# GpSimd sums the softplus of later key blocks: one product with ones per block row in a two-layer decoder trunk

## What is computed

```python
mask = k_pos[None, :] < q_pos[:, None]
z = jnp.einsum('bhqd,bhkd->bhqk', q_blk, k).astype(jnp.float32) * scale
log_beta = jax.nn.log_sigmoid(z)
log_stay = jnp.where(mask, jax.nn.log_sigmoid(-z), 0.0)
log_remain = lax.cumsum(log_stay, axis=3, reverse=True) - log_stay
w = jnp.where(mask, jnp.exp(log_beta + log_remain), 0.0)
return jnp.einsum('bhqk,bhkd->bhqd', w.astype(v.dtype), v)
```

## Time and profile before

| | |
|---|---|
| median of three runs | 4052.87 us |
| the profiled execution | 4055.05 us, of which the span is 4053.0 us |
| TensorE busy (matmuls) | 3955.4 us, 98% of the span |
| VectorE busy | 2637.8 us, 65% |
| ScalarE busy | 1431.2 us, 35% |
| GpSimd busy | 1285.3 us, 32% |
| mean granted TensorE clock | 0.988 of full speed |

### The profile page before, as it was taken

The page is one execution under the profiler, slowest core; times in us unless marked ns, Lnnn a source line. Parts: engine busy times, 40 slices in busy tenths (PEclk is TensorE's granted clock), DMA queues, the critical chain, the costliest instruction groups (busy, mean ns, idle before and its releaser), DMA issues.

```text
span 4053.0 us, 57462 instructions
## 1 busy us (share of the span) xinstructions
PE 3955.4 (98%) x18186; PEld 3240.2 (80%) x18186; DVE 2637.8 (65%) x4343; ACT 1431.2 (35%) x1891; POOL 1285.3 (32%) x869
## 2 busy tenths in 40 slices
PE   8999999999999999999889999999999999999998
PEld 5777878888888878888667777888888888788885
DVE  5742548967774278888566436388777732878784
ACT  4533233333333333333344433333333333333333
POOL 0100003433331077676001000044333310777750
PEclk9999999999999999999999999999999999999999
DMA  3222223445454599999212222234445446999991
GB/s 110 69 87 89 99 78 125 141 158 192 171 186 144 190 341 370 350 356 339 79 64 78 83 93 99 73 131 145 174 171 190 167 146 204 346 366 365 351 322 63
DMA packets 323751, 740.17 MB, mean 183 GB/s; under 512 B 30496, under 2 KB 161696, under 8 KB 319904
## 3 DMA queue, kind: packets, MB, share of 16 engines
q1 hardware_dynamic: 104400, 381.73, 26.9%
q10 hardware_dynamic: 174160, 222.40, 16.2%
q0 software_dynamic: 45056, 134.38, 9.0%
HBM read 618.87 MB, written 119.54 MB: 182 GB/s over the span
## 4 chain that ended last, share of the span: by engine, by line
PE 93%; DVE 2%; issue 2%; ACT 1%; DMA 0%; POOL 0%; ACTq 0%; DVEq 0%; POOLq 0%; SPq 0%
PE bank L1071 60%; PE bank L1279 24%; PE bank L1259 4%; PE bank L1135 1%; PE bank L1125 1%; PE bank L1143 1%; DVE xl L708 1%; PE bank L1092 1%; DVE rs L701 0%; PE bank L1120 0%; PE bank L1214 0%; PE bank L1213 0%; PE bank L1212 0%; DMA vrow<-in_stream,tail_v 0%; ACTq L621 0%
## 5 line engine op out<-in xcount | busy, mean ns | idle before, releaser
L1071 PE MATMUL bank<-xh,hi 128*128 128x512 f32 x3264 | 1311.4, 402 | 42.2 <-DVE xl L708 42.1
L1071 PE MATMUL bank<-xl,hi 128*128 128x512 f32 x3264 | 1277.0, 391 | 0.0
L1071 PE MATMUL bank<-xh,lo 128*128 128x512 f32 x3264 | 1276.4, 391 | 0.0
L696 DVE TENSOR_TENSOR lo<-raw,hi 128x1024 fp32r<-128x1024 f32 (+1 forms) x532 | 642.7, 1208 | 643.4 <-ACT hi L432 596.8
L432 ACT ACTIVATE hi<-raw 128x1024 fp32r<-128x1024 f32 x724 | 739.1, 1044 | 278.9 <-DMA raw<-in_stream 173.9
L380 POOL TENSOR_TENSOR lo<-raw,hi 128x1024 fp32r<-128x1024 f32 x192 | 481.5, 2508 | 1002.4 <-ACT hi L432 1002.2
L1071 PEld LDWEIGHTS bank<-xh,hi 128*128 128x128 f32 x3264 | 616.1, 189 | 194.7 <-DVE xl L708 59.6
L1071 PEld LDWEIGHTS bank<-xh,lo 128*128 128x128 f32 x3264 | 615.9, 189 | 130.6
L1071 PEld LDWEIGHTS bank<-xl,hi 128*128 128x128 f32 x3264 | 617.0, 189 | 120.3 <-issue 3.8
L392 POOL DMA_INDIRECT hval<-early,tail_h x256 | 397.6, 1553 | 428.2 <-DMA early<-eo 347.2
L1279 PE MATMUL bank<-hi,ah 128*128 128x512 f32 x1536 | 475.1, 391 | 12.0 <-DVE al L995 10.3
(11 more groups left out here) (195 smaller groups left out, 3436.6 us busy)
## 6 DMA issues: line engine op xcount, KB each, us to landing
raw<-in_stream SPq DMA_DIRECT2D x724, 512.0 KB
early<-eo ACTq DMA_DIRECT2D x256, 256.0 KB, 2.2
gate_table<-stage ACTq DMA_DIRECT2D x24, 2048.0 KB, 7.4
gb<-gate_table ACTq DMA_DIRECT2D x64, 768.0 KB
eb<-early ACTq DMA_DIRECT2D x64, 768.0 KB
hval<-early,tail_h POOLq DMA_INDIRECT x256
vrow<-in_stream,tail_v POOLq DMA_INDIRECT x256
hT<-in_xT ACTq DMA_DIRECT2D x2, 1024.0 KB, 6.8
```

What stands on the lines that cost most here:

```text
L696: dve.tensor_tensor(lo[k % RING][:, 0:w], raw[k % RAW][:, 0:w], hi[k % RING][:, 0:w].bitcast(f32), ALU.subtract).then_inc(lo_split, 1)
L1071: ins = pe.matmul(out_ap, st[slot][:, a:a + P], mv, start=first and i == 0, stop=last and i == 2)
```

## The change

GpSimd, after its four softplus masks, builds two sums per head: `laterS[1]` (256 columns: block 2 over queries 256 to 383, and blocks 2 + 3 over the last 128) and `laterS[0]` (384 columns: block 1 over queries 128 to 255, and block 1 plus `laterS[1]` over the rest). That is a copy and an add of 128 columns, then a copy of 128 and an add of 256. ScalarE rounds both sums (`laterH`), VectorE takes the rests (`laterL`). TensorE uses them for block rows 1 and 0 in place of one product per later block; rows 3 and 2 are as before. VectorE's `attSl` of blocks 3 and 2 now waits for the first sum and that of block 1 for the second, because it overwrites `attS` that GpSimd still reads.

```diff
--- before.py
+++ after.py
@@ -168,6 +168,9 @@
     attS = sb("attS", o_r + 8 * KB, [P, NBLK, SEQ])
     attW = sb("attW", o_r, [P, NBLK, SEQ])
     attSh = sb("attSh", o_r + 16 * KB, [P, NBLK, SEQ], f32r)
+    laterS = [sb("laterS0", o_r + 6 * KB, [P, 384]), sb("laterS1", o_r + 4 * KB, [P, 256])]
+    laterH = [sb("laterH0", o_r + 22 * KB, [P, 384], f32r), sb("laterH1", o_r + 20 * KB, [P, 256], f32r)]
+    laterL = [sb("laterL0", o_r + 6 * KB, [P, 384], f32r), sb("laterL1", o_r + 4 * KB, [P, 256], f32r)]
     attSl = sb("attSl", o_r + 8 * KB, [P, NBLK, SEQ], f32r)
     qb = sb("qb", o_r + 24 * KB, [P, SEQ])
     kb = sb("kb", o_r + 26 * KB, [P, SEQ])
@@ -267,6 +270,7 @@
         z_ready, abs_ready, ln_ready, sp_ready = sem("z_ready"), sem("abs_ready"), sem("ln_ready"), sem("sp_ready")
         sp_masked, arg_ready, w_ready, w_masked = sem("sp_masked"), sem("arg_ready"), sem("w_ready"), sem("w_masked")
         sp_hi, sp_lo, signs_ready = sem("sp_hi"), sem("sp_lo"), sem("signs_ready")
+        later_ready, later_hi, later_lo = sem("later_ready"), sem("later_hi"), sem("later_lo")
         pv_ready, pv_taken = sem("pv_ready"), sem("pv_taken")
         pooled, pooled_hi, pooled_lo = sem("pooled"), sem("pooled_hi"), sem("pooled_lo")
 
@@ -358,6 +362,16 @@
                         pool.wait_ge(sp_ready, a + i + 1)
                         apart(pool)
                         keep_later(attS, s, sp_masked)
+                    r = l * (4 * PAIRS) + h * 2
+                    pool.wait_ge(sp_masked, a + 3)
+                    apart(pool)
+                    pool.tensor_copy(laterS[1][:, 0:P], attS[:, 2, 2 * P:3 * P])
+                    pool.tensor_tensor(laterS[1][:, P:2 * P], attS[:, 2, 3 * P:SEQ], attS[:, 3, 3 * P:SEQ], ALU.add)\
+                        .then_inc(later_ready, 1)
+                    pool.tensor_copy(laterS[0][:, 0:P], attS[:, 1, P:2 * P])
+                    pool.wait_ge(later_ready, r + 1)
+                    pool.tensor_tensor(laterS[0][:, P:3 * P], attS[:, 1, 2 * P:SEQ], laterS[1][:, :], ALU.add)\
+                        .then_inc(later_ready, 1)
                     for i, s in enumerate(reversed(range(NBLK))):
                         pool.wait_ge(w_ready, a + i + 1)
                         apart(pool)
@@ -493,6 +507,9 @@
                         for i, s in enumerate(reversed(range(NBLK))):
                             act.wait_ge(sp_masked, a + i + 1)
                             act.activation(attSh[:, s, s * P:SEQ], attS[:, s, s * P:SEQ], ACT.Copy).then_inc(sp_hi, 1)
+                        for i in range(2):
+                            act.wait_ge(later_ready, (s2 + h) * 2 + i + 1)
+                            act.activation(laterH[1 - i][:, :], laterS[1 - i][:, :], ACT.Copy).then_inc(later_hi, 1)
                         split(l, 7 if h == 0 else 9, b)
                         if h:
                             act.wait_ge(pooled, l * PAIRS + b + 1)
@@ -768,8 +785,14 @@
                                                      attE[:, s, s * P:SEQ], ALU.max, ALU.add).then_inc(sp_ready, 1)
                         for i, s in enumerate(reversed(range(NBLK))):
                             dve.wait_ge(sp_hi, a + i + 1)
+                            if s:
+                                dve.wait_ge(later_ready, s1 * 4 + h * 2 + (2 if s == 1 else 1))
                             dve.tensor_tensor(attSl[:, s, s * P:SEQ], attS[:, s, s * P:SEQ],
                                               attSh[:, s, s * P:SEQ].bitcast(f32), ALU.subtract).then_inc(sp_lo, 1)
+                        for i in range(2):
+                            dve.wait_ge(later_hi, s1 * 4 + h * 2 + i + 1)
+                            dve.tensor_tensor(laterL[1 - i][:, :], laterS[1 - i][:, :], laterH[1 - i][:, :].bitcast(f32),
+                                              ALU.subtract).then_inc(later_lo, 1)
 
                     def turn_v():
                         dve.wait_ge(v_turned, s1 + 1)
@@ -1130,10 +1153,18 @@
                         a = s1 * 8 + h * 4
                         for i, s in enumerate(reversed(range(NBLK))):
                             pe.wait_ge(sp_lo, a + i + 1)
-                            for j in range(s, NBLK):
+                            for part in (attSh, attSl):
+                                ins = pe.matmul(bank[4 + s][:, s * P:SEQ], tri_r[:, :], part[:, s, s * P:SEQ],
+                                                start=False, stop=True, skip_group_check=True)
+                            if s == 2:
                                 for part in (attSh, attSl):
-                                    ins = pe.matmul(bank[4 + s][:, j * P:SEQ], (tri_r if j == s else ones_r)[:, :],
-                                                    part[:, j, j * P:SEQ], start=False, stop=True, skip_group_check=True)
+                                    ins = pe.matmul(bank[4 + s][:, 3 * P:SEQ], ones_r[:, :], part[:, 3, 3 * P:SEQ],
+                                                    start=False, stop=True, skip_group_check=True)
+                            if s < 2:
+                                pe.wait_ge(later_lo, s1 * 4 + h * 2 + 2 - s)
+                                for part in (laterH, laterL):
+                                    ins = pe.matmul(bank[4 + s][:, (s + 1) * P:SEQ], ones_r[:, :], part[s][:, :],
+                                                    start=False, stop=True, skip_group_check=True)
                             ins.then_inc(arg_ready, 1)
 
                     def weigh(h):
```

## The result

The changed kernel takes 4063.0 us (4060.24 to 4064.28, 11 runs). Beside it the kernel before took 4051.88 us (4050.0 to 4053.78, 11 runs). The ratio is 1.0027 with a 95% interval of 1.0017 to 1.0036: 11.1 us slower, 0.27%. 19.1 us were forecast. The profiled execution took 4061.87 us with a span of 4060.1 us, 7 us more than the profiled one of before. One execution of each says less than eleven, so times are compared by their medians, and the traces are used for where time goes. Followed from product to product, the two traces come 11.4 us apart in the attention, and back by 3.8 us in the stages between.

A forecast was written before the change was run, and what follows sets the result against it. TensorE was taken to bound the kernel, with 93% of the chain. Lateness in `remain`, 16.9 us with the saving counted, plus 2.2 us of `y` waits made 19.1 us slower: 4072.0 us, range 4060 to 4084 us, 8 in 10.

The forecast's parts named there:

- The gain of the products: TensorE's saved products in block rows 1 and 0 of `remain`: 0.57 us a head, 9.1 us in all, the ceiling.
- the step that the prediction called the deciding one: In `remain`, VectorE in order waits for GpSimd's second sum and TensorE for VectorE: 1.10 and 1.01 us late, 16.9 us.
- M: Start of GpSimd's mask of block 0, the last softplus mask of a head: 63.34 in head 0, 79.09 in head 1.
- the rival for the full gain: GpSimd's sums hidden in `remain`, L no later than M + 1.15: 9.1 us faster, about 4044 us; chance 0.02.
- The wait for `y`: TensorE waits for VectorE's `y` at the next pair's mix 0: 0.37 us, 6 times, 2.2 us.
- The clock rival: New waits in the attention bring back the low clock: at most 58 us on top, some 4130 us; chance 0.03.
- L: When VectorE sees GpSimd's second sum and starts `attSl` of block 1 in `remain`: M + 2.78.
- second sum alone: End of GpSimd's second sum for `remain`, with nothing disturbing it: M + 2.49.
- disturbance of GpSimd: GpSimd's copy and add slowed by VectorE's `attSl` of blocks 3 and 2: 0.25 us, bounds 0 and 0.5 us.
- the cheap rival: GpSimd's adds in proportion to columns, copies 0.2 us, no disturbance: L at M + 1.81, about 4056 us; chance 0.12.
- The term behind L: VectorE's remaining rests and TensorE's last products, from L until TensorE leaves `remain`: 2.73 us, at M + 5.51.
- The signs in the trace: TensorE waits in `remain` about 1.6 us a head for `attSl` of block 1 and `laterL[1]`; `remain` lasts about 3.8 us.

The follow-up runs named there:

- The fills: Changed kernel with GpSimd's two copies and two adds per head replaced by two fills with zero, synchronisation kept: 4045.12 us, ratio 0.9984.

## Why the prediction was right in direction and 8 us too dear

**Right.** The gain of the products was of the size predicted (9.1 us against 10.8 measured alone; the saving per head is 0.65 us where its rows gave 0.57), and it was lost at the step that the prediction called the deciding one: VectorE waits for GpSimd's second sum in its order, and TensorE waits for VectorE. The fills show that with that sum at M + 0.91 the gain is there; the rival for the full gain put its point at M + 1.15. The wait for `y` arose six times, as said. `pw` cost nothing. The granted clock did not fall in the attention: it is 1.00 from 63 to 120 us, and the wait of 0.59 us cost 0.06 us of restart. The clock rival's mechanism does exist in this kernel, but at waits of 4.43 us.

The measured 4063.0 us is inside the range given, 3 us from its low end and 9 us from the forecast.

**Wrong: the terms ahead of L.** This is where the sum was mis-sized, and every term of GpSimd's was too high.

| term | predicted | measured |
|---|---|---|
| mask to copy, copy to add | 0.33, 0.33 us | 0.24, 0.27 us |
| add of 128 columns (next start) | 0.62 us | 0.45 us (0.40) |
| second copy (next start) | 0.33 us | 0.25 us |
| add of 256 columns | 0.88 us | 0.77 us |
| second sum alone | M + 2.49 | M + 1.93 |
| disturbance of GpSimd | 0.25 us | 0 |
| VectorE late for the second sum | 0 | 0.18 us |

The straight line through the adds of 512 and 1024 columns gave a fixed part of 0.37 us and 0.62 us for 128 columns; 0.45 us was measured. Two far points don't fix the short end. In proportion to the columns, the cheap rival's way, 0.35 and 0.69 us were too low. The truth lay between, a little nearer to the cheap end. The estimate from the Trainium skill's figure for 2048 elements (GPSIMD Engine Reference, section 3.1) was 0.84 us for both adds. The trace has 1.22 us, so the estimate came 0.38 us too low, and the rows' 1.50 us 0.28 us too high.

**Wrong: who is disturbed.** I charged GpSimd 0.25 us for VectorE's rests of blocks 3 and 2. GpSimd wasn't slowed at all: in all 16 heads its longest second add is 0.79 us. Its add starts at 64.59, the rest of block 2 comes behind it, and that one takes 954 ns where it took 418. TensorE's first wait, 0.25 us, is for just this. The direction follows the order, as the third turn of the choice shows with waits of 4.43 us. The Trainium skill says it outright (SBUF — State Buffer, section Who interferes with whom): VectorE with two inputs in SBUF and GpSimd reading SBUF hold one shared port pair in turn, and whichever issues second "fully blocks". It also says that a GpSimd instruction that only writes doesn't contend. By this rule, the trace agrees: 0.954 us beside the add. Beside the fills the rest of block 3 took 0.292 us and that of block 2, whose start falls into the second fill, 0.418 us, as in the kernel before.

VectorE comes to the rest of block 1 at about 65.58, worked out from the start of `laterL` at 66.65 less the pitches of blocks 0 and 1 (0.61 and 0.46 us). So L was M + 2.15 where I had M + 2.78, 0.63 us too late. The second sum was there at M + 1.93 and seen some 0.04 us later; the last 0.18 us of L are VectorE's own, held up by the drawn-out rest of block 2. The charge of 0.25 us for a disturbance was thus nearly right in size by luck: it stood for a delay of the other engine.

**The term behind L** was nearly right: from 65.58 to 68.44 are 2.86 us, 2.73 us were predicted. The products start more slowly behind the wait (67.20 to 68.44, 1.24 us for 1.12). Together 0.63 - 0.13 = 0.50 us a head, so TensorE left at M + 5.01 and not at M + 5.51. Eight head-0 terms of 0.50 us are 4.0 us and eight head-1 terms of 0.68 us are 5.4 us, 9.4 us in all.

**The `y` wait** was too small, 0.37 us against 0.65 us. TensorE comes 5.88 us after `remain`, at M + 10.71, 0.68 us earlier than forecast, because `remain` was cheaper. `y` ended at M + 11.00 (90.82), and the product started 0.32 us behind its end, at M + 11.32; I had it seen at M + 11.76. A cheaper `remain` made the next wait longer and gave back 6 x 0.28 = 1.7 us. 19.1 - 9.4 + 1.7 = 11.4 us, which is what the account gives.

**The signs in the trace.** Forecast were about 1.6 us of wait a head and a `remain` of 3.8 us; it was 0.66 us of wait in head 0 and 0.47 in head 1, and 3.31 and 3.05 us. The waits named, `attSl` and `laterL`, were the right ones, but the one for `attSl` falls on block 2, not on block 1.

**What stays open.** The pause of VectorE that decides the third turn moves by idle signals; its cause wasn't found. So a part of any difference of 12 us between two versions of this kernel can be this turn. For the change itself that is excluded, since its trace has no wait for `slot`. That the kernel with the sums on VectorE would keep its gain with another count of instructions wasn't tried.

## What to carry over

Work taken off the bounding engine pays only if what replaces it ends before that engine asks: find the latest end that still hides it (here M + 1.15 by the estimate; the runs show that M + 0.91 hides it and M + 1.93 doesn't) before you add up what is saved, and put the new work on the engine that has idle time and the operands at that moment, which here was VectorE and not the idler GpSimd. Where VectorE and GpSimd overlap on SBUF operands, don't charge a share to both: see who starts first, and charge the other the whole rest of the first one's instruction. And before you believe a difference of a few tenths of a per cent, look for waits in stages that the edit doesn't touch, and repeat it with an idle instruction more.

## What the runs showed of the hardware that I had not expected

- Small adds on GpSimd: 0.45 us for 128 columns and 0.77 us for 256, a copy of 128 columns 0.29 us, a fill of 384 columns 0.43 us. The same on VectorE: 0.29, 0.41 and a copy 0.22 us.
- In the overlaps read here the engine that started second did its work behind the other's end: a cast of 0.30 us on VectorE took 2.42 us behind a split on GpSimd that had started 0.12 us before it and ran to 792.51; a split of 2.40 us took 3.77 us behind VectorE.
- Eight increments per pair on VectorE, on which nobody waits, cost 11 us of 4052 in one kernel and gave 12.7 us back in another, through a pause of 0.50 or 0.29 us on VectorE, some 30 us ahead of the wait that it causes.
- A wait of 4.43 us on TensorE left the granted clock at 0.63 for the next 4 us. Waits of up to 0.59 us, two or three a head, left it at 1.00.
